# A mixture-of-experts kernel: the experts' gate and up divided at column 1536 in place of 1408, and the right part of both in one slot

## The reference

```python
logits = t @ w_r + b_r                      # 256 x 8
top_v, top_i = top_k(logits, 2)
gates = one_hot(top_i) * softmax(top_v)
for e in range(8):
    out += gates[:, e] * ((silu(t @ w_g[e]) * (t @ w_u[e])) @ w_d[e])
```

## Time and profile before

| | us |
|---|---|
| median of 3 runs | 1325.21 (1324.31 to 1325.51) |
| profiled execution, its own time | 1323.69 |
| its span, first to last instruction | 1322.2 |
| TensorE busy | 1301.8 (98%) |
| DVE busy | 1006.5 (76%) |
| ACT busy | 827.6 (63%) |

### The profile page before, as it was taken

How to read it: one execution, slowest core, us unless ns; L and a number is a source line. 1 busy time by engine, 2 the same in 40 slices (tenths; PEclk the granted TensorE clock), 3 DMA queues, 4 the chain that set the end, 5 groups by cost and what they waited for, 6 DMA issues and landing times.

```text
span 1322.2 us, 17853 instructions
## 1 busy us (share of the span) xinstructions
PE 1301.8 (98%) x6726; PEld 1062.8 (80%) x6726; DVE 1006.5 (76%) x786; ACT 827.6 (63%) x746; POOL 95.1 (7%) x107
## 2 busy tenths in 40 slices
PE   7999999999999999999999999999999999999998
PEld 6988888888889888877877877778778778778776
DVE  6667764444565777688888888888889788888988
ACT  5555564444455545477777678677677677777674
POOL 4201010000012010200000000000000000000110
PEclk9999999999999999899999999999999999999999
DMA  9633435555599335199999999999999999999994
GB/s 335 200 107 127 156 100 193 195 187 190 189 314 364 101 126 193 62 377 383 350 402 390 345 397 388 359 397 360 384 389 344 395 379 346 412 384 347 411 398 179
DMA packets 117482, 385.26 MB, mean 291 GB/s; under 512 B 6288, under 2 KB 34428, under 8 KB 117436
## 3 DMA queue, kind: packets, MB, share of 16 engines
q1 hardware_dynamic: 105068, 365.08, 73.5%
q10 hardware_dynamic: 9648, 9.84, 2.3%
q0 software_dynamic: 2720, 9.70, 2.2%
HBM read 368.87 MB, written 15.73 MB: 291 GB/s over the span
## 4 chain that ended last, share of the span: by engine, by line
PE 83%; DVE 8%; DMA 3%; ACT 3%; issue 2%; POOL 1%; SPq 0%; DVEq 0%; ACTq 0%
PE bank L1702 34%; PE bank L1698 23%; PE bank L1699 23%; DVE wl L1177 2%; DMA ring<-in_we_gate 2%; DVE wl L1191 2%; ACT wh L819 1%; PE bank L2279 1%; DMA ring<-in_we_up 1%; DVE scratch L1335 1%; DVE scratch L1313 1%; DVE aT_low L1196 1%; POOL mfox L701 0%; PE bank L1723 0%; DMA ring<-in_w_in 0%
## 5 line engine op out<-in xcount | busy, mean ns | idle before, releaser
L1191 DVE TENSOR_TENSOR wl<-ring,wh 128x2816 fp32r<-128x2816 f32 (+1 forms) x127 | 400.4, 3171 | 54.9 <-PE bank L1702 35.4
L819 ACT ACTIVATE wh<-ring 128x2816 fp32r<-128x2816 f32 (+1 forms) x128 | 336.6, 2631 | 149.2 <-DMA ring<-in_we_gate 49.0
L1177 DVE TENSOR_TENSOR wl<-ring,wh 128x2048 fp32r<-128x2048 f32 (+3 forms) x78 | 186.0, 2384 | 120.8 <-ACT wh L805 120.6
L1698 PE MATMUL bank<-wh,xh 128*96 128x512 f32 (+2 forms) x696 | 263.6, 379 | 3.6 <-DVE wl L1191 2.5
L1699 PE MATMUL bank<-wh,xl 128*96 128x512 f32 (+2 forms) x696 | 262.5, 377 | 0.0
L1702 PE MATMUL bank<-wl,xh 128*96 128x512 f32 (+2 forms) x944 | 240.6, 377 | 0.0
L805 ACT ACTIVATE wh<-ring 128x2048 fp32r<-128x2048 f32 (+3 forms) x77 | 152.8, 1984 | 113.7 <-PE bank L1699 100.4
L1191 DVE TENSOR_TENSOR wl<-ring,wh_third 128x2816 fp32r<-128x2816 f32 (+1 forms) x64 | 187.1, 2923 | 30.7 <-PE bank L1702 27.1
L1702 PEld LDWEIGHTS bank<-wl,xh 128*96 128x96 f32 (+1 forms) x944 | 156.8, 166 | 40.3
L819 ACT ACTIVATE wh_third<-ring 128x2816 fp32r<-128x2816 f32 (+1 forms) x64 | 155.4, 2429 | 37.9 <-DMA ring<-in_we_up 16.3
L1698 PEld LDWEIGHTS bank<-wh,xh 128*96 128x96 f32 (+1 forms) x696 | 116.6, 168 | 41.4 <-issue 5.2
(11 more groups left out here) (270 smaller groups left out, 1551.7 us busy)
## 6 DMA issues: line engine op xcount, KB each, us to landing
ring<-in_we_gate SPq DMA_DIRECT2D x64, 1408.0 KB, 7.9
ring<-in_we_up SPq DMA_DIRECT2D x64, 1408.0 KB, 8.0
ring<-in_we_down SPq DMA_DIRECT2D x56, 1536.0 KB, 8.5
ring<-in_w_in SPq DMA_DIRECT2D x8, 1536.0 KB, 14.1
ring<-in_w_gate SPq DMA_DIRECT2D x10, 1024.0 KB, 5.1
ring<-in_w_up SPq DMA_DIRECT2D x10, 1024.0 KB, 5.1
ring<-in_w_down SPq DMA_DIRECT2D x10, 1024.0 KB, 4.9
rows_of<-zeros ACTq DMA_DIRECT2D x1, 9600.0 KB, 64.1
```

The source lines that it names most:

```text
L819: nc.scalar.activation(wh_in_pass(j, n), ring[:, slot, 0:n], ACT.Copy).then_inc(high_ready, 1)
L1177: nc.vector.tensor_tensor(wl[:, j, 0:n], ring[:, slot, 0:n], wh[:, j, 0:n].bitcast(F32), ALU.subtract).then_inc(low_ready, 1)
L1191: nc.vector.tensor_tensor(wl[:, j % 2, 0:n], ring[:, pass_slot(j), 0:n], wh_in_pass(j, n).bitcast(F32), ALU.subtract).then_inc(low_ready, 1)
L1698: nc.tensor.matmul(dst, x_high, w_high, start=first, stop=False)
```

## The change

Gate and up are divided at column 1536 in place of 1408. The left part (LEFT = 1536 columns) keeps the form of half A: fills 0 to 7, gate and up in turn, two groups of channels each, now three full banks of 512 columns. The right part (RIGHT = 1280 columns) of one group of channels holds gate and up side by side in one fill: 2 x 1280 = 5 x 512 columns, eight fills (8 to 15), five banks (gB0, gB1, mB, uB0, uB1). The middle bank mB holds the last 256 columns of gate and the first 256 of up. These fills are two transfers each, one from gate and one from up. The stationary operand of all gate and up products is 128 columns wide (0:P in place of 0:PASS_CAP); columns 96 to 127 of xh and xl are cleared once ahead of the first pass. The transposes, their waits, the banks and the order follow: slots 8 and 9 now stand ahead of the first transposes of A. In the right part only the last fill (15) finishes banks, all five of them.

```diff
-    HALF = DFF // 2
-    HB = -(-HALF // BANK)
-    HT = FT // 2
+    LEFT = 3 * BANK
+    RIGHT = DFF - LEFT
+    HB = 3
+    HT = LEFT // P
+    assert 2 * RIGHT == 5 * BANK
...
-    HBLOCKS = [(0, 4), (4, 4), (8, 3)]
+    HBLOCKS = {"A": [(0, 4), (4, 4), (8, 4)], "B": [(0, 4), (4, 4), (8, 2)]}
+    RIGHT_BLOCKS = ["gB0", "gB1", "mB", "uB0", "uB1"]
+    UP_LAST = {"A": ["uA0", "uA1", "uA2"], "B": ["uB0", "uB1", "uB1"]}
     for n, b in (("gA0", 0), ("gA1", 1), ("gA2", 2), ("uA0", 3), ("uA1", 4), ("uA2", 5),
-                 ("gB0", 6), ("gB1", 7), ("gB2", 0), ("uB0", 1), ("uB1", 2), ("uB2", 3),
-                 ("hA0", 4), ("hA1", 5), ("hA2", 4), ("d0", 4), ("d1", 5),
+                 ("gB0", 6), ("gB1", 7), ("mB", 0), ("uB0", 1), ("uB1", 2),
+                 ("hA0", 3), ("hA1", 4), ("hA2", 5), ("d0", 4), ("d1", 5),
...
-    PASS_PARTS = [1] * PASS_FILLS
+    PASS_PARTS = [1] * KT + [2] * KT + [1] * DSLOT
...
-        PASS_ENDS = {6: "gA2", 7: "uA2", 14: "gB2", 15: "uB2", PASS_FILLS - 1: "d1"}
+        PASS_ENDS = {KT - 2: "gA2", KT - 1: "uA2", 2 * KT - 1: "uB1", PASS_FILLS - 1: "d1"}
...
-            return DFF if j < 2 * KT else min(DROWS, FT - DROWS * (j - 2 * KT)) * D
+            return 2 * LEFT if j < KT else 2 * RIGHT if j < 2 * KT else min(DROWS, FT - DROWS * (j - 2 * KT)) * D
...
-                    c0 = (j // KT) * HALF
-                    src = gu_rows[j % 2][:, bass.ds(e * KT + j % KT // 2 * 2, 2), c0:c0 + HALF]
-                    dst = ring[:, slot, 0:2 * HALF].rearrange("p (k c) -> p k c", k=2)
-                    sp.dma_start(dst, src).then_inc(slot_filled[slot], 16)
+                    if j < KT:
+                        src = gu_rows[j % 2][:, bass.ds(e * KT + j // 2 * 2, 2), 0:LEFT]
+                        dst = ring[:, slot, 0:2 * LEFT].rearrange("p (k c) -> p k c", k=2)
+                        sp.dma_start(dst, src).then_inc(slot_filled[slot], 16)
+                    else:
+                        dst = ring[:, slot, 0:2 * RIGHT].rearrange("p (m c) -> p m c", m=2)
+                        for m in range(2):
+                            sp.dma_start(dst[:, m:m + 1, :], gu_rows[m][:, bass.ds(e * KT + j - KT, 1), LEFT:DFF]
+                                         ).then_inc(slot_filled[slot], 16)
...
+            nc.gpsimd.memset(xh[:, :, PASS_CAP:P].bitcast(F32), 0.0)
+            nc.gpsimd.memset(xl[:, :, PASS_CAP:P].bitcast(F32), 0.0).then_inc(rest_cleared, 1)
...
+                        n = "mB" if (half, i) == ("B", 2) else f"g{half}{i}"
+                        c, w = "AB".index(half) * LEFT + i * BANK, BANK // 2 if n == "mB" else BANK
+                        act.wait_ge(*lfull(n, p))
+                        nc.scalar.activation(h1[0:PASS_CAP, c:c + w], lbank(n)[0:PASS_CAP, 0:w], ACT.Silu
+                                             ).then_inc(gates_out if n == "mB" else ltake(n), 1)
...
+                def up_times_gate(n, at, c0, w):
+                    dve.wait_ge(*lfull(n, p))
+                    h = h1[0:PASS_CAP, c0:c0 + w]
+                    nc.vector.tensor_tensor(h, lbank(n)[0:PASS_CAP, at:at + w], h, ALU.mult).then_inc(ltake(n), 1)
+
+                def left_hidden():
+                    for i in range(HB):
+                        dve.wait_ge(*ltaken(f"gA{i}", p))
+                        up_times_gate(f"uA{i}", 0, i * BANK, BANK)
+
+                def right_hidden():
+                    dve.wait_ge(gates_out, p + 1)
+                    up_times_gate("mB", BANK // 2, LEFT, BANK // 2)
+                    up_times_gate("uB0", 0, LEFT + BANK // 2, BANK)
+                    up_times_gate("uB1", 0, LEFT + BANK // 2 + BANK, BANK)
...
-            pe.wait_ge(rest_cleared, 1)
+            pe.wait_ge(rest_cleared, 2)
...
+                def right_slots(*slots):
                     for j in slots:
-                        s, half = j % KT // 2, "AB"[j // KT]
-                        names = "gu"[j % 2] + half
-                        w_high, w_low = wh_in_pass(j, 2 * HALF), wl[:, j % 2, 0:2 * HALF]
-                        cols = [(i, i * BANK, min(BANK, HALF - i * BANK)) for i in range(HB)]
+                        k, w_high, w_low = j - KT, wh_in_pass(j, 2 * RIGHT), wl[:, j % 2, 0:2 * RIGHT]
+                        pe.wait_ge(high_ready, p * PASS_FILLS + (NSPLIT + j + 1))
+                        if k == KT - 1:
+                            pe.wait_ge(low_ready, p * PASS_FILLS + (NSPLIT + j + 1))
+                            for i, n in enumerate(RIGHT_BLOCKS):
+                                ps, c = lbank(n)[:], i * BANK
+                                ins = both(ps, xh[:, k, 0:P], xl[:, k, 0:P], w_high[:, c:c + BANK], False)
+                                if n == RIGHT_BLOCKS[-1]:
+                                    ins.then_inc(highs_used, 1)
+                                mm(ps, xh[:, k, 0:P], w_low[:, c:c + BANK], False, True).then_inc(ldone(n), 1)
+                            continue
+                        for i, n in enumerate(RIGHT_BLOCKS):
+                            if n == RIGHT_BLOCKS[-1]:
+                                pe.wait_ge(low_ready, p * PASS_FILLS + (NSPLIT + j + 1))
+                            ps, c = lopen(n, p) if k == 0 else lbank(n), i * BANK
+                            ins = both(ps[:], xh[:, k, 0:P], xl[:, k, 0:P], w_high[:, c:c + BANK], k == 0)
+                        ins.then_inc(highs_used, 1)
+                        for i, n in enumerate(RIGHT_BLOCKS):
+                            c = i * BANK
+                            ins = mm(lbank(n)[:], xh[:, k, 0:P], w_low[:, c:c + BANK], False, False)
+                        ins.then_inc(slots_used, 1)
+
+                def left_slots(*slots):
+                    for j in slots:
+                        s, names = j // 2, "gu"[j % 2] + "A"
+                        w_high, w_low = wh_in_pass(j, 2 * LEFT), wl[:, j % 2, 0:2 * LEFT]
                         pe.wait_ge(high_ready, p * PASS_FILLS + (NSPLIT + j + 1))
                         if s < KT // 2 - 1:
                             for k in range(2):
-                                for i, a, n in cols:
+                                for i in range(HB):
                                     if (k, i) == (1, HB - 1):
                                         pe.wait_ge(low_ready, p * PASS_FILLS + (NSPLIT + j + 1))
                                     ps = lopen(f"{names}{i}", p) if s == k == 0 else lbank(f"{names}{i}")
-                                    kk = 2 * s + k
-                                    ins = both(ps[0:PASS_CAP, 0:n], xh[:, kk, 0:PASS_CAP], xl[:, kk, 0:PASS_CAP],
-                                               w_high[:, k * HALF + a:k * HALF + a + n], kk == 0)
+                                    kk, c = 2 * s + k, k * LEFT + i * BANK
+                                    ins = both(ps[:], xh[:, kk, 0:P], xl[:, kk, 0:P], w_high[:, c:c + BANK], kk == 0)
                             ins.then_inc(highs_used, 1)
                             for k in range(2):
-                                for i, a, n in cols:
-                                    ins = mm(lbank(f"{names}{i}")[0:PASS_CAP, 0:n], xh[:, 2 * s + k, 0:PASS_CAP],
-                                             w_low[:, k * HALF + a:k * HALF + a + n], False, False)
+                                for i in range(HB):
+                                    c = k * LEFT + i * BANK
+                                    ins = mm(lbank(f"{names}{i}")[:], xh[:, 2 * s + k, 0:P], w_low[:, c:c + BANK], False, False)
                             ins.then_inc(slots_used, 1)
...
-                        j0, k = HBLOCKS[i]
-                        pe.wait_ge(*ltaken(f"u{half}{i}", p))
+                        j0, k = HBLOCKS[half][i]
+                        pe.wait_ge(*ltaken(UP_LAST[half][i], p))
...
-                gate_up_slots(*range(9))
+                left_slots(*range(KT))
+                right_slots(8, 9)
                 hidden_transposed("A", 0, 1)
-                gate_up_slots(9, 10)
+                right_slots(10)
                 hidden_transposed("A", 2)
-                gate_up_slots(*range(11, 16))
+                right_slots(*range(11, 2 * KT))
```

38 lines of the change are left out of this document (13 added, 25 removed).

## The result

The changed kernel takes **1330.55 us** (median of 22 runs, 1324.90 to 1335.05), the kernel before 1325.16 in the same job (22 runs): ratio **1.0039, 95% interval 1.0030 to 1.0049**. It is 5.4 us slower, where 1320.4 was forecast and the range ended at 1328.5. The profiled execution took 1332.24 us, its span 1330.7, against 1323.69 and 1322.2 before.

A forecast was written before the change was run, and what follows sets the result against it. The expert layer was taken as bound by TensorE, with the DMAs close behind. Products -8.9, start +0.5, slot 6 +1.6 and last pass +2.0 sum to -4.8 us: 1320.4 against the median, range 1315.8 to 1328.5.

The forecast's parts named there:

- Products: Gate and up products on TensorE: 0.2267 us apart, gaining 1.11 us per pass, 8.9 over eight passes.
- A: Rival: gate and up products stay 0.230 apart, the 3.5 ns not being the stationary width's; 1325 us; chance 0.17.
- D: Rival: a product costs its columns alone, so equal columns change nothing; 1325 to 1327 us; chance 0.02.
- Feed: Weight ring at slot 6: fill 6 later by 1.69 us, slot 6 by 1.62; priced 0.2 per pass, 1.6 in all.
- Last pass: Slot 15 of the last pass, beside the row gathers: 1 to 3 us of stall expected, 2.0 taken.
- Start of pass 0: TensorE's wait for xl before the first pass: longer copy and subtraction add 0.5 us, once.
- Priced at nothing: Split issues, clears, conversions and slots 8, 11 and 17: all expected to stay hidden under other work.
- B: Rival: the ring becomes the bound at slots 6 and 15, 2.0 us per pass; 1330 us; chance 0.13.

The follow-up runs named there:

- e5: Changed kernel with the last 128 of 1536 columns left out of each row in the eight left fills; 1321.39 us.
- e16: Changed kernel with gathered_low moved behind subtraction 23 and only one of each pass's 96 result rows written; 1324.46 us.
- e1: Kernel before, old division kept, with gate and up stationaries widened from 96 to 128 columns (added columns cleared once); 1328.15 us.
- e15: Changed kernel, writing only one of the 96 result rows of each pass; 1324.83 us.
- e17: Kernel before, with fills 0 to 7 each bringing 256 more columns (131 KB) in a second transfer that nothing reads; 1342.78 us.
- e6: Kernel before, with fills 8 to 15 issued as two transfers each, same bytes and slots; 1325.55 us.
- e7: Kernel before, plus the two clears of the last 32 columns of xh and xl ahead of the passes; 1324.57 us.

## Why the prediction was wrong

- **(Products)** Right. 0.2267 apart, slots of 4.08 and 3.40. A pass without waits went to 92.63 (e5, e16), against 93.57 and at best 93.43: a gain of 0.8 to 0.94, not 1.11. Of the rest 0.12 stands in slot 0, which takes 4.20. Over eight passes about 7 us in place of 8.9. Rivals A and D are out, though A had a point: by e1 the 3.5 ns come only among neighbours of 512 columns.
- **(Feed)** This step failed: "Fill 6 is ready later by 0.27 (issue), 3 x 0.31 (fills 4, 5, 6), 0.22 (copy) and 0.27 (subtraction) = 1.69 ... So the slack falls by 0.1". For ACT's start on fill 6 the first two terms make 1.20, and the trace has 2.76 on average over seven passes (19.56 against 16.80). The subtraction ends later by 3.1 (25.85 against 22.77), while slot 6, if nothing held it, would come only 1.7 later (24.6 against 22.88). Both terms were too small. The bytes are 1.70 (the changed kernel against e5) and not 0.93: the error is in the count, three fills. In both kernels the transfers pause before fill 1, between 9 and 6 us ahead of the pass, and from there to slot 6 they have one short hole at most, so that six longer fills are in the way, 6 x 0.31 = 1.9. e5 (-9.2 us of time), e15 (-5.3) and e17 (+18.2, fill 6 later by 1.96) show from three sides that such bytes decide. The rest is 1.06 and not 0.27, and 0.98 of it is there at fill 3 already; the issue of fill 0, 13.4 us ahead of a pass on average where it was 13.9, is a part of that, and the rest of it stays open. The text even said "up to 0.3 where fills 1 to 3, also longer, are still in the way", and priced it far too low: fill 3 is 2.4 late. The limit for ACT's start moved by 1.2 (17.0 to 18.2), so the slack fell by 2.76 - 1.2, about 1.5 us a pass, and not by 0.1; on average there had been 17.0 - 16.8 = 0.2.
- **(Last pass)** Priced at +2.0 beside 0.2 for slot 6. Its listed waits grew by 3.1, from 0.59 at slot 6 and 0.21 at slot 15 to 2.08 and 1.81: slot 15 as priced (1.6 more), slot 6 not (1.5 more). With the products' gain in it the pass is 2.6 longer.
- **(Start of pass 0)** Priced at +0.5; the wait grew from 1.13 to 1.45. What was not priced: the clock behind it. TensorE's first product and a stretch behind it:

```profile
566.52 0.54 PE L1717 MATMUL bank<-wh,xh 128*128 128x512 f32 x1 [1.45 <-DVE xl L1209]
```

```profile
568.00:570.00 2.00, 2.00 (x6) 1.52 (x6) 1.08 (x1) 2.00 (x2) 0.00 (x0) 0.50 1.02 409
```

  About 1.7 us, in 4 of the 11 profiles with the new division (after waits of 1.45, 1.46, 1.59 and one shorter) and in none of the 9 with the old one.
- **(Priced at nothing)** Right: split issues (e6), clears (e7), slots 8, 11 and 17, apart from 0.4 and 0.6 us at slot 17 in two passes. The conversions of 2560 columns took 2.35 and 2.82 us, as worked out.
- **(Rivals)** B, the feed, is what happened, and its deciding point, fills more than about 1 us late, is passed by fill 6 in all seven passes from 660.73 on. That its 1330 is the measured 1330.55 is luck in part: it took 1.3 us a pass at slot 6, which came close (0.6 to 2.1 in six passes), but also 0.7 a pass at slot 15 for the split fills, where only the last pass waits and where e6 shows no cost of the split. Two things spoke for it and were weighed too lightly: the DMA share of 0.96 to 0.98 over whole passes, and the late fill of the earlier trace rows, which showed that 2 us of lateness already made a wait of 1.2. The argument against it, 216 GB/s from 735 to 745, was of another stretch: a hole there gives nothing back to slot 6.

As a sum, in this profile, from start to start: -8.9 for the products, +13.6 (17.8 less 4.2) for all that the gate and up slots take beyond them, +0.9 in the down slots, slot 17 above all: 5.6, where the eight passes are 5.5 us longer. In the 13.6 are 1.7 of clock and 1.0 for slot 0; the rest, some 11, is lateness of the feed, where 3.6 had been priced. The listed waits, +7.9 (10.4 less 2.5), show only part of it.

## What to carry to other kernels

Where the transfers are nearly always busy (here a share of 0.96 to 0.98 over whole passes), bytes that a re-division moves to the front of a pass count for every fill between the last hole of the queue and the slot in question, not for the few that are issued in the pass. Work out when each fill must be there and when it is, before counting what TensorE saves. A list of waits shows less than the waits cost; compare starts with starts. And test a step's price in the kernel that it is for: the same move of one instruction group was worth -3.3 us in one division and +6.0 in the other.
